# An encoder layer on eight cores: the order of the last stage, DFT tiles in the first stage's planner, and sums and multiplications moved between engines

## The reference

```
h = rms_norm(x);  proj = h @ w_in -> u (256), q, k, v (768 each), two gates (1024 each)
branch A: u -> real part of the 2-D DFT over (2048 positions, 64 channels of a group) -> a 64x64 map per group
branch B: windowed attention, 3 groups of 4 heads with (window, dilation) = (128,1), (512,4), (2048,16),
          rotary on the first 16 dims of a head; the groups combined by their softmax denominators
x += (sigmoid(g_f) * (A @ w_f) + sigmoid(g_a) * (B @ w_a)) @ w_mix_out
x += cross_attention(rms_norm(x), rms_norm(mem))        # 256 memory tokens, 4 heads
x += relu(rms_norm(x) @ w_up)**2 @ w_down               # 4096 hidden channels
out = rms_norm(x)
```

## Time and profile before

| | us |
|---|---|
| median of 3 runs (lowest, highest) | 2020.15 (1993.32, 2088.87) |
| the profiled execution | 1995.15 |
| its span, slowest core (core 5) | 1994.1 |
| spans of the eight cores | 1987.8 to 1994.1 |
| TensorE, VectorE, ScalarE, GpSimd busy | 1957.0, 963.5, 773.3, 417.5 |

### The profile page before, as it was taken

How to read it: one execution, slowest core, us unless ns; L and a number is a source line. 1 busy time by engine, 2 the same in 40 slices (tenths; PEclk the granted TensorE clock), 3 DMA queues, 4 the chain that set the end, 5 groups by cost and what they waited for, 6 DMA issues and landing times.

```text
span 1994.1 us, 30646 instructions; the slowest of 8 cores (1987.8 to 1994.1 us)
## 1 busy us (share of the span) xinstructions
PE 1957.0 (98%) x10234; PEld 968.8 (49%) x10234; DVE 963.5 (48%) x1585; ACT 773.3 (39%) x1291; POOL 417.5 (21%) x384
## 2 busy tenths in 40 slices
PE   8999999999999999999999999999999999999996
PEld 4456544554444444444445664446444444444443
DVE  5955643455553333336764456335556332323355
ACT  6355742455431332213325557235554112021243
POOL 3001042531310321101420002344133000000034
PEclk9999999999999999999999999999999999999998
DMA  9472352663012525043372440635600040222112
GB/s 239 85 138 64 54 139 73 106 110 60 1 64 43 118 69 110 22 79 116 102 198 60 86 81 23 189 59 96 121 1 1 1 79 6 46 40 43 22 75 95
DMA packets 51738, 155.41 MB, mean 78 GB/s; under 512 B 4993, under 2 KB 15362, under 8 KB 42114
## 3 DMA queue, kind: packets, MB, share of 16 engines
q0 software_dynamic: 14416, 75.50, 22.2%
q1 hardware_dynamic: 37026, 77.94, 12.6%
q10 hardware_dynamic: 144, 0.02, 0.0%
HBM read 205.87 MB, written 16.78 MB: 112 GB/s over the span
## 4 chain that ended last, share of the span: by engine, by line
PE 93%; DVE 2%; SPq 1%; DMA 1%; issue 1%; ACT 1%; POOL 0%; DVEq 0%; ACTq 0%; POOLq 0%
PE ps L149 93%; DVE arena L149 2%; SPq L149 1%; DMA arena<-x 1%; ACT arena L149 1%; DMA arena<-arena 0%; POOL arena L149 0%; SPq L147 0%; DVEq L143 0%; ACTq L143 0%; POOLq L143 0%; SPq L143 0%
## 5 line engine op out<-in xcount | busy, mean ns | idle before, releaser
L149 PE MATMUL ps<-arena 128*128 128x512 bf16 (+4 forms) x10234 | 1957.0, 354 | 28.9 <-ACT arena L149 12.0
L149 PEld LDWEIGHTS ps<-arena 128*128 128x128 bf16 (+1 forms) x10234 | 968.8, 100 | 1016.8 <-issue 70.1
L149 ACT ACTIVATE arena<-ps 128x512 bf16<-128x512 f32 (+3 forms) x776 | 472.4, 631 | 869.7 <-PE ps L149 747.7
L149 DVE TENSOR_TENSOR arena<-arena 128x512 bf16<-128x512 bf16 (+8 forms) x597 | 305.9, 532 | 479.3 <-ACT arena L149 466.5
L149 POOL TENSOR_TENSOR arena<-arena 128x512 f32<-128x512 f32 (+2 forms) x289 | 358.2, 1242 | 697.4 <-ACT arena L149 484.5
L149 DVE TENSOR_TENSOR arena<-ps,arena 128x512 f32<-128x512 f32 (+4 forms) x394 | 280.2, 722 | 280.2 <-PE ps L149 270.6
L149 ACT ACTIVATE arena<-arena 128x512 f32<-128x512 f32 (+6 forms) x460 | 282.4, 625 | 299.8 <-DVE arena L149 198.3
L149 DVE SCALAR_TENSOR_TENSOR arena<-arena 128x512 bf16<-128x512 f32 (+3 forms) x312 | 215.6, 730 | 37.8 <-ACT arena L149 37.3
L149 POOL DMA_DIRECT2D arena<-wb x62 | 33.8, 547 | 641.2 <-PE ps L149 602.7
L149 DVE SCALAR_TENSOR_TENSOR arena<-arena,ps 128x512 f32<-128x512 f32 x128 | 80.6, 683 | 126.9 <-PE ps L149 121.3
L149 DVE SCALAR_TENSOR_TENSOR arena<-ps,arena 128x512 f32<-128x512 f32 x64 | 43.5, 687 | 32.9 <-PE ps L149 32.9
(11 more groups left out here) (4 smaller groups left out, 0.4 us busy)
## 6 DMA issues: line engine op xcount, KB each, us to landing
arena<-wb POOLq DMA_DIRECT2D x62, 1024.0 KB, 9.9
arena<-x SPq DMA_DIRECT2D x8, 2048.0 KB, 24.5
arena<-x SPq DMA_DIRECT2D x32, 512.0 KB, 3.8
out<-arena SPq DMA_DIRECT2D x28, 512.0 KB, 2.8
arena<-wa POOLq DMA_DIRECT2D x17, 512.0 KB, 9.5
arena<-x SPq DMA_DIRECT2D x32, 256.0 KB, 14.7
arena<-rope SPq DMA_DIRECT2D x6, 1024.0 KB, 6.4
arena<-arena SPq DMA_DIRECT2D x96, 64.0 KB, 2.3
```

Source lines behind the costliest of these rows:

```text
L149: ins = getattr(eo, o['name'])(*o['args'], **o['kw'])
```

## The change

It has five parts. (1) The end: in the last sequence `up(3, tg + 1)` comes before `down(3, tg)` only for groups 0 and 1; `up(3, 3)` comes behind `down(3, 2)`. The first half of the last `down` issues seven of the eight matmuls of two tiles ahead (`late`). The last chunk's square of the first half, and the last three of the second, are not added by GpSimd: they go into the sum over channels as float32 matmuls (`direct`). Steps are taken later and one at a time. (2) The DFT of the first sequence becomes planner jobs, split into matmuls (`z`, `d`, `zx`, `mid`) and evictions; `make_wz` becomes three jobs; the order of the bank users changes (V tiles 4 and 5 before group 3's tiles). (3) GpSimd also adds chunk 7 of each group's odd chain, and one fold add per channel half in both sequences. (4) Half of group 1's normalised copies move from the planner to `rest`, which now does one per tile, twelve in all; `mem_gen` waits 12 steps instead of 21. (5) The projections of group 1 in the first sequence go by token group (3, 0, 1, 2) with q and k of each together, and the gather of q and a weight load (`aload(8)`) move from tile 7 to tile 13.

```diff
-        def norm_sq(k, src, n=512, ns=0, eng='pool', lag=False, bufs=None):
+        ones32_ = view(OFF['Y'] + 12 * KB, 128, F32)
+        sq_last = [[view(OFF['Y'] + (3 * i + k) * KB, 256, F32) for k in range(3)] for i in range(2)]
+        def norm_sq(k, src, n=512, ns=0, bufs=None, direct=0):
...
+            def split():
                 act(hi, acc_, AF.Copy)
                 tt('dve', lo, acc_, hi, ALU.subtract)
+            if k == (6 if direct == 3 else 8):
+                split()
+            if k >= 8 - direct:
+                act(sq_last[ns][k - 8 + direct][:, 0:n], src, AF.Square)
+            elif k:
+                act(sq_, src, AF.Square)
+                tt('pool', acc_, acc_, sq_, ALU.add)
+            else:
+                act(acc_, src, AF.Square)
+            if k == 7 and direct < 3:
+                split()
...
+            mm(o, ones, lo[:, 0:n], False, direct == 0)
+            for k in range(direct):
+                mm(o, ones32_, sq_last[ns][k][:, 0:n], False, k == direct - 1)
...
-                    tt('dve', fold[:, 3, j, 0:511], o[:, 1:512], o[:, 1023:512:-1], ALU.add)
+                    tt('pool', fold[:, 3, j, 0:511], o[:, 1:512], o[:, 1023:512:-1], ALU.add)
...
+                PADD = (3, 5, 7)
-                        tt('pool' if c in (3, 5) else 'dve', p_, p_, sc[c % 4], ALU.add)
+                        tt('pool' if c in PADD else 'dve', p_, p_, sc[c % 4], ALU.add)
...
+                turns = o_(0, 1) + w_(0, 4) + o_(2) + w_(4, 6) + o_(3) + w_(6, 8) + [('zo', n, 0) for n in range(4)] + [('zxo',)] + \
+                        [('do', 0, odd, part) for odd in range(2) for part in (1, 0)] + [('zo', n, 1) for n in range(4)] + \
+                        [('do', 1, odd, part) for odd in range(2) for part in (1, 0)] + [('mido',)]
...
-                    for c in range(8):
-                        job(('n', tg, c), 'dve', 0.7, 55.0 + tg, lambda tg=tg, c=c: apply(tg, c),
+                    for c in range(8 - 4 * tg):
+                        job(('n', tg, c), 'dve', 0.7, 41.5 + 14 * tg, lambda tg=tg, c=c: apply(tg, c),
...
-                    job(('f', j), 'dve', 5.2, 40.0 + 5 * j, lambda j=j: folds(j), [('o', tg, j) for tg in range(NTG)])
-                job('wz', 'dve', 1.5, 35.0, make_wz, [('r', NTG - 1, 0)])
+                    job(('f', j), 'dve', 5.4, 40.0 + 5 * j, lambda j=j: folds(j), [('o', tg, j) for tg in range(NTG)] + [('n', 0, c) for c in range(8)])
+                job(('wz', 0), 'dve', 0.2, 35.0, lambda: make_wz(0), [('r', NTG - 1, 0)])
+                job(('wz', 1), 'pe', 0.25, 35.0, lambda: make_wz(1), [('wz', 0)])
+                job(('wz', 2), 'dve', 0.8, 35.0, lambda: make_wz(2), [('wz', 1)])
...
+                for j in range(2):
+                    for n in range(4):
+                        b, prev = turn('zo', n, j)
+                        job(('z', n, j), 'pe', 0.25, 46.0 + 4 * j, lambda n=n, j=j, b=b: z_mm(n, j, b), [('f', j), ('wz', 2), prev] + [('f', 1 - j)][:0])
+                        job(('zo', n, j), 'act', 0.6, 46.0 + 4 * j, lambda n=n, j=j, b=b: z_out(n, j, b), [('z', n, j)])
+                    for odd in range(2):
+                        for im in (1, 0):
+                            b, prev = turn('do', j, odd, im)
+                            due = 60.0 + 4 * j + 2 * odd
+                            job(('d', j, odd, im), 'pe', 0.9, due, lambda a=(j, odd, im, b): dft_mm(*a),
+                                [('zo', n, j) for n in range(4)] + ['dftl', ('zxo',), prev])
+                            job(('do', j, odd, im), *((('act', 0.6) if im else ('dve', 1.4))), due, lambda a=(j, odd, im, b): dft_out(*a),
+                                [('d', j, odd, im)] + [('do', j, odd, 1)] * (1 - im) + [('n', 1, c) for c in range(4)])
...
                 def rest():
-                    for c in range(8):
-                        apply(RAW - 1, c)
-                        if c in (2, 5, 7):
+                    for tg in range(1, RAW):
+                        for c in range(8 - 4 * tg if tg < RAW - 1 else 0, 8):
+                            apply(tg, c)
                             yield
...
-                    which, c, tg = n // 8, (n // 4) % 2, (n - 1) % 4
+                    by_tg = b_ == 0 and g == 1
+                    which, c, tg = (n % 4 // 2, n % 2, (3, 0, 1, 2)[n // 4]) if by_tg else (n // 8, (n // 4) % 2, (n - 1) % 4)
...
-                    if n == 7:
+                    if n == (13 if by_tg else 7):
                         gather(g, 0)
...
-            def down(p_, tg, t0=0, n=512):
+            def down(p_, tg, t0=0, n=512, ns=0, first=None, direct=0):
...
+                late = direct == 1
+                def tile_mm(fc, dcs):
+                    if fc not in bank:
+                        bank[fc] = P.bank()
+                    w = bslot(17 + 4 * p_ + fc // 4).rearrange("p (k j) -> p k j", k=8)
+                    for dc in dcs:
+                        mm(psf(bank[fc])[:, 0:n], w[:, dc, (fc % 4) * 128:(fc % 4 + 1) * 128], a2T[tg % 2][:, dc, tn], dc == 0, dc == 7)
+                if late:
+                    for fc in range(2):
+                        tile_mm(fc, range(7))
                 for fc in range(8):
+                    tile_mm(fc, (7,) if late and fc < 2 else range(8))
...
+                    popp(fc, first, 1 if direct else 2)
...
+            if last_seq:
+                OP('dve', 'memset', ones32_, 1.0, writes=[ones32_])
+                up(3, 0)
+                for tg in range(NTG - 1):
+                    if tg < NTG - 2:
+                        up(3, tg + 1)
+                    down(3, tg)
+                    pend.append(fin_out(tg))
+                up(3, 3)
+                for k, direct in enumerate((1, 3)):
+                    down(3, 3, 256 * k, 256, k, 3, direct)
+                    pend.append(fin_out(3, 256 * k, 256, k, direct))
+                flush()
+                continue
```

More of the change, by code:

```diff
@@ L445, in build_program @@
             ALLB = (0, 1, 2, 3, 4, 5, 6, 7)
-            FB = (6, 7)
+            FB = (7, 6)
             DB = (2, 3, 6, 7, 4, 5)
@@ L590, in mem_gen @@
                 dma('sp', memst, dr['mem'][b_].rearrange("p (c m) -> p c m", c=8), 'mem')
-                for _ in range(21):
+                for _ in range(12):
                     yield
@@ L814, in build_program, with in_bank @@
                     v_unit(0, 2 * i, ALLB)
-            zx_unit()
-            for j in range(2):
-                for i in range(4):
-                    z_unit(i, j)
-            for j in range(2):
-                for odd in range(2):
-                    dft_unit(j, odd, DB)
-            dft_mid((4,))
+                def in_bank(bank, mm_, out, *a):
+                    b = P.bank(bank)
+                    mm_(*a, b)
+                    out(*a, b)
+                in_bank((0,), zx_mm, zx_out)
+                for j in range(2):
+                    for i in range(4):
+                        in_bank(((2, 3, 6, 7), (1, 4, 5, 0))[j][i:i + 1], z_mm, z_out, i, j)
+                for j in range(2):
+                    for odd in range(2):
+                        for part in (1, 0):
+                            in_bank(DB, dft_mm, dft_out, j, odd, part)
+                in_bank((4,), mid_mm, mid_out)
             v_ones(1)
@@ L1207, in up @@
             def up(p_, tg, hook=None):
-                first = 1 + last_seq if p_ == 3 else 6 if p_ + tg == 0 else 3
+                first = (4 if tg == 3 else 2) if p_ == 3 and last_seq else 1 if p_ == 3 else 6 if p_ + tg == 0 else 3
                 for fc in range(8):
@@ L1333, in build_program @@
                     pend.append(fin_out(tg - 1))
[L1334 to L1345 removed]
+            down(3, 3)
+            flush()
+            pend.append(fin_out(3))
+            load_rope(0)
+            for i in range(4, 8):
+                aload(i)
         sems = []
```

128 lines of the change are left out of this document (56 added, 72 removed).

## The result

| | before | after |
|---|---|---|
| median, us (lowest, highest) | 2007.09 (1993.32, 2088.87), 4 runs | 1983.06 (1980.97, 1984.43), 4 runs |
| the profiled execution, us | 1995.15 | 1984.43 |
| span, slowest core (all cores), us | 1994.1 (1987.8 to 1994.1) | 1983.4 (1976.6 to 1983.4) |
| mean span of the eight cores, us | 1990.3 | 1978.8 |

The ratio is 0.9946, interval 0.9922 to 0.997: 5 of 1000 shorter, clear of 1 but far under 2%. 1980 was forecast, 15.3 less than the profiled execution; the profiled one after is 10.7 less, the mean span 11.5.

A forecast was written before the change was run, and what follows sets the result against it. TensorE was taken as busy nearly throughout, with gains only in stage 1 (VectorE's) and the last 37.1 us (a chain of waits). End 10.3 + stage 1 4.0 + projections 1.0 = 15.3 off 1995.15 gave 1980 us, range 1970 to 2003.

The forecast's parts named there:

- The end, 10.3: Last down tiles to the kernel's end: reordering, float32 sums and later steps save 10.3 us, from 6 to 12.
- the seam: Passage from `up(3, 3)` to `down(3, 3)`: a wait between 0 and 5.2 us, taken as 1.0.
- The tail behind the last matmul: After the last matmul: add's lag saves 1.1, square to Ln 1.85, stores cost 0.5; together 2.4 us.
- (b): Rival at the end: the seam costs its 5.2 us and the clock falls behind it; 1985.5 us, chance 0.12.
- (d): Rival at the end: the stores set it, so the new end does nothing; 1990 us, chance 0.03.
- Stage 1, 4.0: Stage 1, its DFT and attention's first visits: TensorE's waits and half its lost clock go, less GpSimd's cost; 4.0 us saved.
- the projections' 1.0: Projections beside attention: moving a gather and a weight load shortens the 2.07 us wait for the second gather; 1.0 us saved.
- rival (a): Stage 1 stays VectorE's, its relief returning through GpSimd's adds or other waits; stage and projections bring nothing; 1985 us, chance 0.20.
- (c): Rival: the planner's order makes z or DFT tiles wait for folds, costing 13.8 to 15.9 us; 2000.8 us, chance 0.08.
- GpSimd's adds, -0.65: Stage 1: four operations moved to GpSimd relieve VectorE but lengthen its instructions; between -1.4 and +2.8 us, taken as -0.65.
- The applies, 1.1: Norm multiplications spread one to a tile beside attention: TensorE's waits of 0.56, 0.28 and 0.29 us go, 1.1 us saved.
- signs of being right: After 1940 us no TensorE wait over 1 us but one at the seam, full clock; no `make_wz` wait; shorter gather wait.

The follow-up runs named there:

- end2: The changed kernel with the second half's norm subtraction queued one chunk later and group 2's norm taken one tile later in `up(3, 3)`; median 1981.88 us, ratio 0.9939.
- no_f32: The changed kernel with all squares added by GpSimd and no float32 matmuls in the norm sums; mean span 1980.9 us, last stretch 2.45 us longer.
- wz_only: The kernel before with only `make_wz` split into three planner jobs; mean span 1988.8 us against 1990.3 before.
- no_pool: The changed kernel with the chunk 7 adds and fold adds moved from GpSimd back to VectorE; ratio 0.9942 to before.
- late_rot: The changed kernel with the rotations of groups 1 and 2 started two V tiles later in both sequences; lowest run 1995.45 us, mean span 1991.9.
- late_load: The changed kernel with two weight loads of group 1 placed after V tiles 5 and 6 in the program; mean span 1978.0 us against 1978.8.

## Why the prediction was partly right and partly wrong

**The end, 10.3: right, 9.4, in part by luck.** Of this the body, up to the last matmul, was to give 7.9, and gave 8.0: about 9.0 in the last stretch, of which 1.0 came back ahead of it, where `up(3, 3)` now meets the norm of group 2. That norm was put at nothing and the seam, which costs 0.3, at 1.0, so two errors nearly cancel. 0.6 of the 1.0 was one number (`first`), as end2 shows. The tail behind the last matmul was to give 2.4 and gave 1.4. From the square's end to the Ln it was 1.7 (from 2.65 to 0.91; 1.85 forecast), and no_f32 prices this step at 2.45 with all that hangs on it. The lag of the last add was to shrink by 1.1, and grew from 1.4 to 1.7, since the subtraction stands ahead of it: the prediction counted VectorE's multiplications and not a wait in its queue. The stores cost 0.1, not 0.5. Rivals (b) and (d) are out: the seam doesn't cost 5.2, and the clock stays up behind it.

**Stage 1, 4.0: this step failed**, and with the projections' 1.0 it brought 1.6 (0.8 before a0 and 0.8 from there to a1; the other 0.5 of the 2.1 is the second sequence's). The 4.0 summed up TensorE's waits, each at its full length: 1.83, 1.1, 0.87, and 0.85 of clock. The waits did go, as said. But the sum took VectorE to have room, at one place in words ("if VectorE has room") and in no number. wz_only takes 0.8 off the waits for the 1.83; the 0.87 at the DFT is in its place 0.39, 0.41 and 0.65 on core 3, after 1.28, 0.43 and 0.60 at the z tiles; and the clock, of which half was to come back, fell on five of eight cores behind these new waits. Its 1.7 us had been read on core 5; of the other seven only core 3 had any lower clock between 44 and 107 us before, so the mean of all had 0.85 us at the lower level, half of it lost, and has 2.13 now. This is rival (a), with (c)'s mechanism at a sixth of (c)'s price: the z tiles do wait for the second fold, some 2.3 us and not 13.8. What the runs showed in place of the sum stands in VectorE's timeline of after: first and second fold, shuffle, the rest of the rotation and the DFT's adds from 71.78 to 97.11 us, with one pause of 0.94 among the rows shown.

```profile
71.78 3.23 DVE L149 TENSOR_TENSOR arena<-arena 128x1023 f32<-128x1023 f32 x4 [1.32 <-ACT arena L149]
...
77.74 4.31 DVE L149 TENSOR_TENSOR arena<-arena 128x1023 f32<-128x1023 f32 x4
...
84.03 2.29 DVE L149 STREAM_SHUFFLE arena<-arena 128x2048 bf16<-128x2048 bf16 x1
86.49 3.69 DVE L149 TENSOR_TENSOR arena<-arena 128x2048 bf16<-128x2048 bf16 x3 [0.17 <-DVE arena L149]
90.21 2.98 DVE L149 TENSOR_TENSOR arena<-ps,arena 128x512 bf16<-128x512 f32 x4
94.13 2.98 DVE L149 TENSOR_TENSOR arena<-ps,arena 128x512 bf16<-128x512 f32 x4 [0.94 <-ACT arena L149]
```

TensorE meets these links in turn. With the first wait dodged and the second's work taken away 3.1 us come; with one of the two nearly nothing.

**GpSimd's adds, -0.65: no such loss was seen.** The stretch is real, 0.77 and 0.82 us on the two adds shown, against the 1.05 taken from the earlier trace rows. The trace agrees with the rule of the Trainium skill ("SBUF — State Buffer", "SBUF: two separate sides") that the prediction names: each of these two adds ends 0.55 us after the GpSimd add beside it. But no_pool shows that to take the four operations away gains nothing that can be seen in stage 1 and costs 0.25 in the second sequence. The prediction priced a longer instruction as lost time without asking what then waits for it.

**The applies, 1.1:** no multiplication is waited for after 99 us (waits between 99 and 107 fell from 0.65 to 0.04 in the mean), and a0 to a1 became 0.8 shorter. **The projections' 1.0** is then mostly not there: the wait for the second gather fell by 0.4 on the slowest cores and 0.2 in the mean between 125 and 200 us. late_rot says that a later shuffle only moves the wait; late_load left the loads where they were, so whether they slow the gathers, and what makes the last transfer take 6.7 us, stays open. **The second sequence**, costed at nothing, gained 0.5 before its attention, 0.25 of it by the fold add on GpSimd.

Its signs of being right came but for a wait of 1.09 us in the last norm, where none over 1 was to be, and that of being wrong, a wait of several us before the z or DFT tiles, came as 2.3 us. VectorE's busy time in the stage did not grow. The chance of 0.91 for within 2% fitted: the idle time that there was could give no more.

## What to carry to other kernels

In a stage where a second engine is busy nine tenths of the time, don't add up the waits of the first: remove the wait and see in the second engine's row which of its instructions comes next, and price the gain as the distance between the two. A change that gives nothing alone may be half of one that does, where two chains bind in turn; test them together before dropping either. See in the trace that an experiment moved what it was to move before reading its time (late_load didn't), and read a clock on every core, not on the slowest alone. At the end of a kernel the reverse holds: nothing comes after it, and the sum of the links that were taken out comes near the gain, as long as every instruction ahead of the last link in its queue was counted, the waiting ones too.

## What the runs showed of the hardware

A GpSimd add of two SBUF inputs lengthens a VectorE add of the same kind from 0.69 to some 1.5 us (and, in after on core 3 at 53.46 us, two multiplications from 1.40 to 2.42 us), and in this kernel that still came out about even. Behind waits of 1.28, 0.43 and 0.60 us within 3 us the clock fell to the lower level on five of eight cores and held on three, with the same instructions, so the same waits cost a core either nothing more or some 1.7 us (worked out from 2.13 us at the lower level in the mean of eight cores, half of it lost); the cores' a0 in after lie between 95.6 and 97.3.
